# Mixer tokens ordered by 16 grid columns, and neighborhood tiles on 2 or 3 key blocks instead of 4

## The chip, the core and the metric

The kernel runs on one core of one Trainium2 chip. Its engines are TensorE (PE in the profile; its weight loads are PEld), VectorE (DVE), ScalarE (ACT), GpSimd (POOL) and SyncE (SP), which issues the weight loads from memory. The metric is the device time of the core in microseconds, lower is better.

## What is computed

Two blocks of a network on 512 tokens of width 1024, in float32. The first block (attention with a forget gate, a recurrent branch, then a mixture of experts) is not touched by the change. The second block has two layers, each with a mixer and a feed-forward part. The mixer is what matters here. Its tokens are a grid of 8 rows by 64 columns, token = 64 row + column. It has three branches:

```python
def neighborhood_attention(q, k, v, rpb):          # 6 heads of 64
    rows = S // GRID_W                             # 8 rows, GRID_W = 64
    kh = min(NA_KH, rows)                          # 8: all rows
    col_start = jnp.clip(cols - kw // 2, 0, GRID_W - kw)   # kw = 16 columns
    col_idx = col_start[:, None] + jnp.arange(kw)[None, :]
    ...
    s = jnp.einsum('bhqd,bhrqcd->bhqrc', q_row, k_win) * scale + bias
    p = softmax over the 8 x 16 keys of the window
    return jnp.einsum('bhqrc,bhrqcd->bhqd', p, v_win)

def dilated_attention(q, k, v):                    # 6 heads, 3 groups: (128, 1), (512, 4), (2048, 16)
    offs = dilation * jnp.arange(-half, half + 1)  # keys at token distance offs, bias -slope * |offs|
def memory_attention(q, mem_n, w_kv):              # 4 heads, 256 memory tokens

h = rms_norm_2(x, g_pre_mix[l]); proj = h @ w_in[l]
merged = sum over branches of sigmoid(gate) * (branch output @ branch weight)
x = x + rms_norm_2(merged @ w_out[l], g_post_mix[l])
h = rms_norm_2(x, g_pre_ffn[l])                    # then up, conv over 3 tokens, gelu gate, down
```

A query in column c sees all 8 rows but only 16 columns, so with the tokens in order of rows each block of 128 queries (two rows) has some key in every block of 128 keys.

## The kernel before

Activations lie with features on the 128 partitions and tokens in the free dimension: `x`, `h`, `low`, `y` are [128, 8, 512]. A layer is the body of a loop over `LAYERS` = 2 (phase `L`), written out on each engine by hand; the order of each engine's instructions is the order of the code, and engines meet at semaphores only (`Signal`).

A layer begins with the norm `pre_mix`: ScalarE issues the loads of `lvec` (L1241) and of the first bias `nab` (L1242) and squares `x` (L993), TensorE sums (L674), VectorE scales into `low` (`rms_apply`, L1392), ScalarE copies the rounded high part into `h_r` (`high`, L1053) and VectorE forms the rest, `low_r` (`low_part`, L1511). Then come the products for q, k, v. `residual` (L1398, L1401) adds the mixer's output to `x` after the branches, and the feed-forward part follows, whose convolution needs the tokens in their natural order.

Between these stands the attention of the three branches, 24 neighborhood tiles (`na`: 6 heads by 4 blocks of 128 queries), then 8 dilated (`dil`) and 16 memory tiles (`mem`), in the list `TILES["L"]`. `key_chunks(kind, t)` gives the number of key blocks of 128: 4, 6 and 2. The engines are pipelined over tiles. In its round i TensorE issues the score product of tile i (L704, or L701 for `dil`), the transposes of the probabilities of tile i-2, one each block (L715), a product or two of a gate (`gate_products`, L951, 128x512, one in the rounds of `na` tiles and two later), and the value products of tile i-3 (L729). VectorE does for tile i-1 the reciprocal of the row sum (L1432), for tile i the addition of the bias with the row minimum (L1455 for `na`, L1458 and L1460 for `dil`), and for tile i-2 the copy of the transposes out of PSUM (L1474). ScalarE does the exp (L1015), with the row sum read out behind it, and the copy of a finished pair of heads out of PSUM (L1029). GpSimd multiplies the probabilities by the reciprocal (L1861). A score product of tile i waits until the scores of tile i-2 are read; the transposes of a tile wait for GpSimd.

The bias of a head is loaded by ScalarE's queue (L1268) one head ahead into one of two halves of `nab`, [128, 896]. GpSimd then adds the mask of the column window to it (L1900). The four query tiles read it at shifts of 128 columns, 512 wide. The dilated bias of group 0 is read the same way, as 512 neighbours from 3 - t on.

The first block has an attention of its own (phase `A`, kind `fa`) through the same function: 8 heads by 4 query blocks with 1, 2, 3 and 4 key blocks, and no gate products between; every fourth tile a product of L807 for the next head but one.

## Time and profile before

| what | us |
|---|---|
| median of 3 runs | 2861.29 |
| lowest, highest | 2856.5, 2867.2 |
| span of the profiled execution | 2863.9 |
| TensorE busy in it | 2580.2 (90%) |
| VectorE, ScalarE, GpSimd busy | 1157.0, 801.4, 161.5 |

The page gives for the profiled execution its span, from the first to the last instruction; no other time of that execution is shown. Times in the rows further down count from the start of the span. PEclk is the granted clock of TensorE: 1.00 is 2.4 GHz and 0.50 is 1.2 GHz, its two levels. A float32 product shows as two matmul records, and the records of one kind that follow each other are merged with their count. In a row of a timeline the first number is the start, the second the duration; the ends of matmuls are modelled, so what one step takes is read from its start to the start of the next. In layer 0 the neighborhood tiles stand from 1164 to 1238 us, in layer 1 from 2089 to 2163.

### The profile page before, as it was taken

To read this page: it belongs to the slowest core of one execution; us is meant where nothing else is said; L and a number is where in the kernel's file an instruction comes from. 1 tells how busy PE (TensorE), PEld (TensorE's weight loads), DVE (VectorE), ACT (ScalarE), POOL (GpSimd) and SP (SyncE) were. 2 spreads that over 40 slices of the span, in tenths; PEclk is the share of its full clock that TensorE was granted. 3 is DMA by queue.
4 is the path that set the end of the run, shared out by engine and by line. 5 is a ranking of instruction groups with operands and counts; after the bars stand their busy time and mean duration, and the time that the engine had idled before them with its cause. 6 is when DMAs were issued, how large, how long until landed. Compare 5 with 4: busy or idle time off the path is not lost.

```text
span 2863.9 us, 30233 instructions
## 1 busy us (share of the span) xinstructions
PE 2580.2 (90%) x11744; PEld 1956.3 (68%) x11744; DVE 1157.0 (40%) x1664; ACT 801.4 (28%) x1110; POOL 161.5 (6%) x165
## 2 busy tenths in 40 slices
PE   5899886899999489999997999978999999799996
PEld 3674464677777258666875888856866787588885
DVE  5635564000000431354346655333135434655533
ACT  3432313010000142233233433313223323433331
POOL 0001100000000100331000000000033100000000
PEclk8995596899999789899998999989989999899998
DMA  6535041688888413101221222221210122122221
GB/s 238 191 117 206 1 179 50 254 317 319 316 313 311 185 54 117 41 7 59 89 103 45 102 97 95 103 75 67 103 48 1 70 93 88 59 94 98 103 89 45
DMA packets 55809, 353.75 MB, mean 124 GB/s; under 512 B 6016, under 2 KB 6656, under 8 KB 19328
## 3 DMA queue, kind: packets, MB, share of 16 engines
q1 hardware_dynamic: 40464, 294.67, 27.8%
q10 hardware_dynamic: 8640, 30.08, 2.8%
q0 software_dynamic: 6576, 27.26, 2.4%
q8 instruction: 83, 1.36, 0.2%
q14 instruction: 46, 0.38, 0.0%
HBM read 319.49 MB, written 32.51 MB: 123 GB/s over the span
## 4 chain that ended last, share of the span: by engine, by line
PE 44%; issue 40%; DVE 4%; POOL 2%; ACT 2%; DMA 1%; POOLq 0%; DVEq 0%; ACTq 0%
PE lin L870 9%; PE lin L629 7%; PE lin L630 6%; PE lin L643 5%; PE lin L882 5%; PE attn L729 3%; PE score L704 2%; PE trans L715 2%; PE lin L634 2%; POOL y L1861 1%; DVE rstd L1375 1%; PE sums L674 1%; PE sums L669 1%; PE score L701 1%; PE lin L807 0%
## 5 line engine op out<-in xcount | busy, mean ns | idle before, releaser
L629 PE MATMUL lin<-h_r,ring_r 128*128 128x512 f32 x1584 | 626.7, 396 | 46.5 <-ACT h_r L1053 35.7
L630 PE MATMUL lin<-h_r,ring_r 128*128 128x512 f32 x1584 | 622.0, 393 | 0.0
L1505 DVE TENSOR_TENSOR ring_r<-ring,ring_r 128x2048 fp32r<-128x2048 f32 x138 | 316.2, 2292 | 559.1 <-ACT ring_r L1049 559.0
L629 PEld LDWEIGHTS lin<-h_r,ring_r 128*128 128x128 f32 x1584 | 301.0, 190 | 123.7 <-ACT h_r L1053 31.0
L643 PE MATMUL lin<-low_r,ring_r 128*128 128x512 f32 x1392 | 350.1, 391 | 1.9
L630 PEld LDWEIGHTS lin<-h_r,ring_r 128*128 128x128 f32 x1584 | 301.4, 190 | 62.0
L1049 ACT CAST ring_r<-ring 128x2048 fp32r<-128x2048 f32 x138 | 262.4, 1902 | 166.1 <-PE lin L634 105.5
L643 PEld LDWEIGHTS lin<-low_r,ring_r 128*128 128x128 f32 x1392 | 261.3, 188 | 63.2 <-DVE low_r L1511 9.8
L870 PEld LDWEIGHTS lin<-y,ring 128*128 128x128 f32 x2304 | 262.6, 194 | 11.0 <-issue 11.0
L870 PE MATMUL lin<-y,ring 128*128 128x128 f32 x2304 | 263.0, 277 | 2.1 <-DVE y L1741 1.1
L1327 ACT ACTIVATE ob<-lin,lvec 128x512 f32<-128x512 f32 x88 | 68.7, 781 | 301.6 <-PE lin L643 243.7
L1832 DVE SCALAR_TENSOR_TENSOR ob<-lin,lvec,ob 128x511 f32<-128x511 f32 x88 | 66.0, 750 | 196.5 <-ACT ob L1327 194.6
L882 PE MATMUL lin<-ring,ob 128*128 128x512 f32 x288 | 132.8, 604 | 12.0 <-DVE ob L1735 7.8
L1735 DVE TENSOR_TENSOR ob<-gat,lin 128x512 f32<-128x512 f32 x18 | 12.4, 689 | 317.2 <-PE lin L870 317.2
L634 PE MATMUL lin<-big_r,ring_r 128*128 128x512 f32 x352 | 137.2, 390 | 0.6 <-DVE big_r L1511 0.6
L704 PE MATMUL score<-big 64*128 64x512 f32 (+3 forms) x224 | 127.6, 660 | 6.7 <-DVE stat L1455 4.5
L1861 POOL TENSOR_TENSOR y<-y,stat 128x512 f32<-128x512 f32 (+2 forms) x96 | 93.2, 970 | 498.8 <-DVE stat L1432 498.5
L674 PE MATMUL sums<-h,ones_d 128*128 128x512 f32 x96 | 57.9, 760 | 56.9 <-ACT h L993 51.8
L729 PE MATMUL attn<-y,big 128*64 128x128 f32 x704 | 103.3, 286 | 0.0
L882 PEld LDWEIGHTS lin<-ring,ob 128*128 128x128 f32 x288 | 51.7, 189 | 71.8 <-issue 54.7
L729 PEld LDWEIGHTS attn<-y,big 128*64 128x64 f32 x704 | 76.5, 140 | 31.9 <-issue 31.9
L1432 DVE RECIPROCAL stat<-stat 128x1 f32<-128x1 f32 x128 | 20.9, 164 | 184.6 <-PE score L704 133.7
(287 smaller groups left out, 3151.5 us busy)
## 6 DMA issues: line engine op xcount, KB each, us to landing
ring<-in_weights SPq DMA_DIRECT2D x281, 1024.0 KB, 4.9
slots_in<-nab POOLq DMA_DIRECT2D x1, 13312.0 KB, 42.6
y<-slots_in ACTq DMA_DIRECT2D x20, 512.0 KB, 3.6
slots_out<-ob ACTq DMA_DIRECT2D x18, 512.0 KB, 8.7
nab<-in_na_bias ACTq DMA_DIRECT2D x12, 448.0 KB, 3.3
slots_out<-nab POOLq DMA_DIRECT2D x1, 3072.0 KB, 48.4
x<-in_xT ACTq DMA_DIRECT2D x1, 2048.0 KB, 10.9
outT<-x POOLq DMA_DIRECT2D x1, 2048.0 KB, 6.6
```

Of the source, the lines that this page charges most:

```text
L629: pe.matmul(acc, wh, high(k), start=(k == 0), stop=False)
L630: mm = pe.matmul(acc, wl, high(k), start=False, stop=False)
L634: mm = pe.matmul(acc, wh, low(k), start=False, stop=(k == kb - 1))
L643: mm = pe.matmul(acc, wh, low(k), start=False, stop=(k == kb - 1))
L674: mm = pe.matmul(sums[:, 0, 0:n], ones[:, :], src, start=(k == 0), stop=(k == n_k - 1))
L704: mm = pe.matmul(score[:, i % 2, 0:n], q_of(kind)[lo:lo + DH, hp, t * P:(t + 1) * P], k_of(kind)[lo:lo + DH, hp, 0:n], start=True, stop=True)
L729: mm = pe.matmul(attn[lo:lo + DH, o % 2, t * P:(t + 1) * P], v_of(kind, hp, half, t, c0 + c), probsT[name][j % 2][:, c * P:(c + 1) * P], s ...
L870: mm = pe.matmul(acc[:, m * P:(m + 1) * P], wblock(ph, n0 + m * KB + k), xg[e % 2][:, k, :], start=(k == 0), stop=(k == KB - 1))
L882: mm = pe.matmul(acc, hid[e % 2][:, k * P:(k + 1) * P], wblock(ph, n0 + k * KB + 4 * i, 4 * P), start=(k == 0), stop=(k == EB - 1))
L1049: act.copy(ring_r[:, HIGH_SLOT[ph.name][c], :], ring[:, slot, :]).then_inc(*w_high.on(ph, c))
L1505: dve.tensor_tensor(ring_r[:, slot, :], ring[:, slot, :], whole(ring_r[:, HIGH_SLOT[ph.name][c], :]), ALU.subtract).then_inc(*w_low.on(ph, c))
L1861: pool.tensor_tensor(p, p, stat[:, 2, i % 4:i % 4 + 1].to_broadcast([P, n]), ALU.mult).then_inc(*p_ready.on(ph, i))
```

## The change

Within the mixer a token's place becomes 32 a + 4 r + x for row r and column 4 a + x, so a block of 128 places holds 16 columns of all 8 rows. The normed input is written to `y` and brought to the new order by the casts to `h_r` and the subtractions to `low_r` (`by_column`, `by_row`: the same buffer with its free dimension split in three and walked in another order, runs of four words). The residual addition after the mixer brings it back. q, k, v and all branch outputs in between are in the new order.

A query block t of a neighborhood tile now needs the key blocks `NA_KEYS[t]`: from block 0 two, from 0 three, from 1 three, from 2 two. Score product, bias addition, exp, scaling, transposes, copy and value products of the tile are that wide. The bias is stored for three kinds of tile side by side, 2 + 3 + 2 blocks, 896 columns again, with the mask already in it, so GpSimd's addition goes and VectorE waits for the load itself. The dilated bias of group 0 is stored as 128 groups of 7, of which a tile reads 4 each; that of the other groups is loaded once each layer into `tmp`. Small constants (`wf`, `wr`, `route_b`) move into `nab`, which is free until the layers.

```diff
@@ -143,9 +143,29 @@
 }
 
 
+NA_KEYS = [(0, 2), (0, 3), (1, 3), (2, 2)]
+NA_BIAS = [0, 2 * P, 2 * P, 5 * P]
+NA_W = 7 * P
+
+
 def key_chunks(kind, t):
 
-    return {"fa": t + 1, "na": 4, "dil": 6, "mem": 2}[kind]
+    return {"fa": t + 1, "na": NA_KEYS[t][1], "dil": 6, "mem": 2}[kind]
+
+
+def first_key(kind, t):
+
+    return NA_KEYS[t][0] if kind == "na" else 0
+
+
+def by_column(ap):
+
+    return ap.rearrange("p (a r x) -> p r a x", r=ROWS, x=4)
+
+
+def by_row(ap):
+
+    return ap.rearrange("p (r a x) -> p r a x", r=ROWS, x=4)
 
         big, big_r = sb_parts("big", [P, FB, S])
         ob, ob_r = sb_parts("ob", [P, 6, S])
         mem = sb("mem", [P, KB, N_MEM])
-        nab = sb("nab", [P, 2, NA_SLOTS * GRID_W])
-        dil = sb("dil", [P, 2, DIL_W])
+        nab = sb("nab", [P, 2, NA_W])
+        dil = sb("dil", [P, 2, DIL_NEAR])
         tmp = sb("tmp", [P, 2, S])
         gat = sb("gat", [P, 2, S])
         sd = sb("sd", [P, S])
         rstd = sb("rstd", [P, S])
-        consts = sb("consts", [P, 3 * P + GRID_W + 48])
+        consts = sb("consts", [P, 3 * P + 48])
         ones_d = sb("ones_d", [P, P])
         ones = sb("ones", [P, P])
         vec = sb("vec", [P, N_VEC])
         lvec = sb("lvec", [P, N_LVEC])
-        wf = sb("wf", [P, KB, HEADS])
-        wr = sb("wr", [P, KB, N_GROUPS + EXPERTS])
-        route_b = sb("route_b", [P, TT * 20])
+        nab_flat = nab[:, :, :].rearrange("p a b -> p (a b)")
+        wf = nab_flat[:, D:D + KB * HEADS].rearrange("p (a b) -> p a b", a=KB)
+        wr = nab_flat[:, D + 64:D + 224].rearrange("p (a b) -> p a b", a=KB)
+        route_b = nab_flat[:, D + 224:D + 224 + TT * 20]
+        dil_far = tmp[:, 0, :].rearrange("p (a b) -> p a b", a=2)
         slots = sb("slots", [P, 2 * TT], U32)
         weight = sb("weight", [P, 2 * TT])
...
@@ -701,8 +719,9 @@
                             mm = pe.matmul(o, q, k, start=True, stop=True)
                     else:
                         n = key_chunks(kind, t) * P
+                        k0 = first_key(kind, t) * P
                         mm = pe.matmul(score[:, i % 2, 0:n], q_of(kind)[lo:lo + DH, hp, t * P:(t + 1) * P],
-                                       k_of(kind)[lo:lo + DH, hp, 0:n], start=True, stop=True)
+                                       k_of(kind)[lo:lo + DH, hp, k0:k0 + n], start=True, stop=True)
                     mm.then_inc(*qk_done.on(ph, i))
 
                 def turn(j):
@@ -726,7 +745,7 @@
                     total = key_chunks(kind, t)
                     lo = DH * half
                     for c in range(n):
-                        mm = pe.matmul(attn[lo:lo + DH, o % 2, t * P:(t + 1) * P], v_of(kind, hp, half, t, c0 + c),
+                        mm = pe.matmul(attn[lo:lo + DH, o % 2, t * P:(t + 1) * P], v_of(kind, hp, half, t, first_key(kind, t) + c0 + c),
                                        probsT[name][j % 2][:, c * P:(c + 1) * P],
                                        start=(c0 + c == 0), stop=(c0 + c == total - 1))
                     mm.then_inc(*pv_done.on(ph, j))
@@ -1236,9 +1255,13 @@
                 def normed_parts(st):
                     for k in range(KB):
                         act.wait_ge(*normed.by(ph, (st, k)))
-                        high(ph, st, k, h_r[:, k, :], low[:, k, :])
+                        if st == "pre_mix":
+                            high(ph, st, k, by_column(h_r[:, k, :]), by_row(y[:, k, :]))
+                        else:
+                            high(ph, st, k, h_r[:, k, :], low[:, k, :])
 
                 act.dma_start(lvec[:, :], lvec_in[l]).then_inc(lvec_s, 16)
+                act.dma_start(dil_far, far_in).then_inc(far_s, 16)
                 act.dma_start(nab[:, 0, :], na_bias_in[l * NA_HEADS]).then_inc(nab_s, 16)
                 for k in range(KB):
                     square(ph, "pre_mix", k, x[:, k, :], h[:, k, :])
@@ -1398,7 +1421,11 @@
                     dve.scalar_tensor_tensor(tmp[:, k % 2, :], src[:, k, :], lv(g, k), rstd[:, :], ALU.mult,
                                              ALU.mult).then_inc(*upd.on(ph, (st, k)))
                     dve.wait_ge(*upd.by(ph, (st, k)))
-                    dve.tensor_tensor(x[:, k, :], x[:, k, :], tmp[:, k % 2, :], ALU.add).then_inc(*x_new.on(ph, (st, k)))
+                    if st == "post_mix":
+                        dve.tensor_tensor(by_row(x[:, k, :]), by_row(x[:, k, :]), by_column(tmp[:, k % 2, :]),
+                                          ALU.add).then_inc(*x_new.on(ph, (st, k)))
+                    else:
+                        dve.tensor_tensor(x[:, k, :], x[:, k, :], tmp[:, k % 2, :], ALU.add).then_inc(*x_new.on(ph, (st, k)))
 
             ada_chunks = {g[1:]: c for c, g in enumerate(LAST_USE["A"][::PER_CHUNK]) if g[0] == "ada"}
@@ -1450,14 +1477,15 @@
                         dve.tensor_scalar(nm, nm, -1.0, None, ALU.mult).then_inc(*scored.on(ph, i))
                     elif kind == "na":
                         hd = 2 * hp + half
-                        lo = (2 * TT - 2 - 2 * t) * GRID_W
-
-                        dve.tensor_tensor_reduce(p[:, 0:n], s, nab[:, hd % 2, lo:lo + S], -1.0, BIG, ALU.add, ALU.min,
-                                                 nm).then_inc(*scored.on(ph, i))
+                        lo = NA_BIAS[t]
+                        dve.tensor_tensor_reduce(p[:, 0:n], s[:, 0:n], nab[:, hd % 2, lo:lo + n], -1.0, BIG, ALU.add,
+                                                 ALU.min, nm).then_inc(*scored.on(ph, i))
                     elif kind == "dil":
-                        dve.tensor_tensor_reduce(p[:, 0:S], score_flat[:, 0:S], dil[:, half, 3 - t:3 - t + S], -1.0, BIG,
+                        near = dil[:, half, :].rearrange("p (a x) -> p a x", x=7)[:, :, 3 - t:7 - t]
+                        dve.tensor_tensor_reduce(p[:, 0:S].rearrange("p (a x) -> p a x", x=4),
+                                                 score_flat[:, 0:S].rearrange("p (a x) -> p a x", x=4), near, -1.0, BIG,
                                                  ALU.add, ALU.min, nm).then_inc(*score_step.on(ph, (i, 0)))
-                        dve.tensor_tensor_reduce(p[:, S:n], score_flat[:, S:n], dil[:, half, S + 3:], -1.0, BIG,
+                        dve.tensor_tensor_reduce(p[:, S:n], score_flat[:, S:n], dil_far[:, half, :], -1.0, BIG,
                                                  ALU.add, ALU.min, far).then_inc(*score_step.on(ph, (i, 1)))
                         dve.wait_ge(*score_step.by(ph, (i, 1)))
                         dve.tensor_tensor(nm, nm, far, ALU.min).then_inc(*scored.on(ph, i))
@@ -1479,10 +1507,12 @@
                         kind = tl[i][0]
                         dve.wait_ge(*qk_done.by(ph, i))
                         if kind == "na" and i % TT == 0:
-                            dve.wait_ge(*nab_ready.by(ph, i // TT))
+                            dve.wait_ge(nab_s, ph.reg * (16 * NA_HEADS) + 16 * (i // TT + 1))
                         if kind == "fa" and i % TT == 0:
                             hd = i // TT
                             dve.wait_ge(*lin_free[bank_of["A"][f"nc{hd}"]].by(A, f"nc{hd}"))
+                        if i == NA_TILES and name == "L":
+                            dve.wait_ge(far_s, ph.reg * 16 + 16)
                         if i >= 3 and kind != "mem":
                             dve.wait_ge(*t_done.by(ph, ROUNDS_OF[name][i - 3][-1]))
                     if 1 <= i <= n:
@@ -1769,9 +1799,14 @@
                 ph = Phase("L", l)
 
                 def normed_parts(st, g):
-                    rms_apply(ph, st, lambda k: low[:, k, :], lambda k: x[:, k, :], lambda k: lv(g, k), KB)
-                    for k in range(KB):
-                        low_part(ph, st, k, low_r[:, k, :], low[:, k, :], h_r[:, k, :])
+                    if st == "pre_mix":
+                        rms_apply(ph, st, lambda k: y[:, k, :], lambda k: x[:, k, :], lambda k: lv(g, k), KB)
+                        for k in range(KB):
+                            low_part(ph, st, k, by_column(low_r[:, k, :]), by_row(y[:, k, :]), by_column(h_r[:, k, :]))
+                    else:
+                        rms_apply(ph, st, lambda k: low[:, k, :], lambda k: x[:, k, :], lambda k: lv(g, k), KB)
+                        for k in range(KB):
+                            low_part(ph, st, k, low_r[:, k, :], low[:, k, :], h_r[:, k, :])
                 def add_squares(st, k, square, former):
 
...
@@ -1892,20 +1925,7 @@
                         slots[:, i * TT + t:i * TT + t + 1], 0)).then_inc(picked_in[t], 16)
             pool.wait_ge(consts_in, 16 * 4)
             with pool.Fori(0, LAYERS) as l:
-                ph = Phase("L", l)
-
-                def bias(hd):
-                    b = nab[:, hd % 2, :].rearrange("p (a b) -> p a b", b=GRID_W)
-                    pool.wait_ge(nab_s, l * (16 * NA_HEADS) + 16 * (hd + 1))
-                    pool.tensor_tensor(b, b, window.unsqueeze(1).to_broadcast([P, NA_SLOTS, GRID_W]),
-                                       ALU.add).then_inc(*nab_ready.on(ph, hd))
-
-                def next_bias(i):
-                    if i == 0:
-                        bias(0)
-                    if i % TT == 2 and i // TT + 1 < NA_HEADS:
-                        bias(i // TT + 1)
-                attention(ph, extra=next_bias)
+                attention(Phase("L", l))
 
 
+            out.append(np.where(ok, -slopes[2 * g + b] * np.abs(dist).astype(np.float32), np.float32(MASKED)))
+    return np.stack([out[0], out[3]], axis=1), np.stack([out[1], out[2], out[4], out[5]], axis=1).reshape(P, 2, DIL_FAR)
 
 
 def neighborhood_bias(rpb):
 
 
-    c = np.arange(GRID_W)
-    reach = 2 * NA_KW - 1
-    pad = np.zeros((*rpb.shape[:3], 2 * GRID_W - 1), np.float32)
-    lo = GRID_W - 1 - (NA_KW - 1)
-    pad[..., lo:lo + reach] = rpb
-    full = pad[..., GRID_W - 1 + c[None, :] - c[:, None]]
-    full = full.transpose(0, 1, 3, 2, 4)
-    both = np.concatenate([full[:, :, :, 1:], full[:, :, :, :-1]], axis=2)
-    return np.ascontiguousarray(both).reshape(-1, P, NA_SLOTS * GRID_W)
+    tiles = []
+    for t in (0, 1, 3):
+        c0, n = NA_KEYS[t]
+        col, row = (v[:, None] for v in columns(np.arange(t * P, (t + 1) * P)))
+        key_col, key_row = (v[None, :] for v in columns(np.arange(c0 * P, (c0 + n) * P)))
+        start = np.clip(col - NA_KW // 2, 0, GRID_W - NA_KW)
+        inside = (key_col >= start) & (key_col < start + NA_KW)
+        across = np.where(inside, key_col - col + NA_KW - 1, 0)
+        tiles.append(np.where(inside, rpb[:, :, key_row - row + NA_KH - 1, across], np.float32(MASKED)))
+    return np.ascontiguousarray(np.concatenate(tiles, axis=-1)).reshape(-1, P, NA_W)
 
 
```

On TensorE, in the rounds of neighborhood tiles away from the ends, one round before (`lin` is the bank of the gate, `ring_r` its weights, `attn` the value products' bank; L695 and L713 are waits on a register's value):

```order
L704 MATMUL score<-big 128x512
L713 REGISTER_ALU
L715 MATMUL trans<-consts,y 128x128 x4
L951 MATMUL lin<-h_r,ring_r 128x512
L729 MATMUL attn<-y,big 64x128 x4
L695 REGISTER_ALU
```

and two rounds of the change at the same place, tiles with three key blocks in the score product:

```order
L723 MATMUL score<-big 128x384
L732 REGISTER_ALU
L734 MATMUL trans<-consts,y 128x128 x2
L970 MATMUL lin<-h_r,ring_r 128x512
L748 MATMUL attn<-y,big 64x128 x3
L713 REGISTER_ALU
L723 MATMUL score<-big 128x384
L732 REGISTER_ALU
L734 MATMUL trans<-consts,y 128x128 x2
L970 MATMUL lin<-h_r,ring_r 128x512
L748 MATMUL attn<-y,big 64x128 x2
```

No instruction changes its place; the products are narrower and there are fewer transposes and value products.

On ScalarE, at the start of a layer, before (`h` takes the squares of `x`):

```order
L1241 DMA lvec<-in_lvec 128x232
L1242 ISA
L1242 DMA nab<-in_na_bias 128x896
L993 ACTIVATE h<-x 128x512 x8
```

and in the change:

```order
L1263 DMA lvec<-in_lvec 128x232
L1264 DMA tmp<-in_dil_far 128x512
L1265 ISA
L1265 DMA nab<-in_na_bias 128x896
L1012 ACTIVATE h<-x 128x512 x8
```

One load has come in ahead of the squares.

## Rows read from the trace of the kernel before

**Rows 1.** The page, its header: the span of the profiled execution.
```profile
span 2863.9 us, 30233 instructions
```

**Rows 2.** Stretches: start:end, length, busy us (instructions) of PE, PEld, DVE, ACT, POOL, clock.
```profile
214.00:339.00 125.00, 117.48 (x304) 59.88 (x304) 71.69 (x197) 27.41 (x75) 23.07 (x32) 0.50 0.30 121
...
1166.00:1182.00 16.00, 13.38 (x34) 6.91 (x34) 7.79 (x19) 5.08 (x11) 6.19 (x5) 0.50 0.20 73
1183.00:1237.00 54.00, 54.00 (x280) 31.95 (x280) 25.49 (x76) 15.72 (x39) 27.42 (x23) 1.00 0.10 31
```

**Rows 3.** Timeline (start, us, engine, line, tiles), one neighborhood round at full clock.
```profile
1185.85 1.12 PE L704 MATMUL score<-big 64*128 64x512 f32 x2
...
1186.90 0.66 PE L715 MATMUL trans<-consts,y 128*128 128x128 f32 x4
...
1187.09 0.67 DVE L1455 CUSTOM_DVE_ANT_0 y<-score,nab 128x512 f32<-128x512 f32 x1
...
1187.31 0.48 PE L951 MATMUL lin<-h_r,ring_r 128*128 128x512 f32 x1
...
1187.72 1.09 PE L729 MATMUL attn<-y,big 128*64 128x128 f32 x8
1187.80 0.72 ACT L1015 ACTIVATE y<-y,stat 128x512 f32<-128x512 f32 x1 [2.08 <-DVE stat L1455]
...
1188.43 0.19 ACT L1015 ACTIVATION_READ_ACCUMULATOR y<-y,stat 128x1 f32 x1
...
1188.74 1.12 PE L704 MATMUL score<-big 64*128 64x512 f32 x2
```

**Rows 4.** Timeline, TensorE, one memory round (two key blocks) at full clock.
```profile
1290.87 0.70 PE L704 MATMUL score<-big 64*128 64x256 f32 x2
...
1291.49 0.44 PE L715 MATMUL trans<-consts,y 128*128 128x128 f32 x2
...
1291.69 0.71 PE L951 MATMUL lin<-low_r,ring_r 128*128 128x512 f32 x2
...
1292.33 0.65 PE L729 MATMUL attn<-y,big 128*64 128x128 f32 x4
...
1292.91 0.70 PE L704 MATMUL score<-big 64*128 64x256 f32 x2
```

**Rows 5.** Timeline, TensorE, neighborhood rounds at the lower clock.
```profile
1168.70 2.07 PE L704 MATMUL score<-big 64*128 64x512 f32 x2 [2.46 <-DVE stat L1455]
...
1174.41 1.11 PE L715 MATMUL trans<-consts,y 128*128 128x128 f32 x4
...
1177.78 2.07 PE L704 MATMUL score<-big 64*128 64x512 f32 x2
1179.78 1.11 PE L715 MATMUL trans<-consts,y 128*128 128x128 f32 x4
```

**Rows 6.** Timeline, TensorE, first block's attention: a score product of three blocks.
```profile
298.19 1.65 PE L704 MATMUL score<-big 64*128 64x384 f32 x2
...
299.76 0.47 PE L715 MATMUL trans<-consts,ob 128*128 128x128 f32 x1
```

**Rows 7.** Timeline: the first transposes of the stage and the first dilated score product.
```profile
1170.93 1.11 PE L715 MATMUL trans<-consts,y 128*128 128x128 f32 x4 [0.16 <-POOL y L1861]
...
1237.82 2.17 PE L701 MATMUL score<-big 64*128 64x512 f32 x6
```

**Rows 8.** Timeline: the issue of the first bias load at the layer's start.
```profile
1008.21 0.35 ACTq L1242 DMA_DIRECT2D nab<-in_na_bias  x1
```

**Rows 9.** Copies of attention outputs in the layers: ns min/median/max, first and last start.
```profile
L1029 ACT COPY ob<-attn x12: 564/577/1063, 1203.0 to 2247.3; 128x512 f32<-128x512 f32 x12
```

**Rows 10.** Groups by form: the residual additions, busy us and mean ns.
```profile
L1401 DVE TENSOR_TENSOR x<-x,tmp 128x512 f32<-128x512 f32 x32 | 22.1, 692 | 1.1
```

**Rows 11.** Timeline, layer 0: the eight casts and eight low parts of pre_mix.
```profile
1024.39 5.26 ACT L1053 CAST h_r<-low 128x512 fp32r<-128x512 f32 x8 [4.21 <-DVE low L1392]
...
1028.92 4.89 DVE L1511 TENSOR_TENSOR low_r<-low,h_r 128x512 fp32r<-128x512 f32 x8
```

49 lines of the change are left out of this document (21 added, 28 removed).

## Prediction

> **What bounds the kernel now.** I read the page's header first, for the span [rows 1], then a table of stretches with the granted clock [rows 2], then the instructions of single tiles in order of time. The change acts on the mixer, which runs twice. In the neighborhood stage of one layer TensorE is busy 54.00 of 54.00 us at full clock, with VectorE at 25.49, ScalarE at 15.72 and GpSimd at 27.42 [rows 2]. So what TensorE issues there sets the time, and work taken from the other three is worth nothing by itself. The second thing to see is the clock. It is at 0.50 when the stage begins (16 us from 1166) and is 1.00 from 1183 on, so it came back between 1182 and 1183. And in the first block's attention, 214 to 339 us, it stays at 0.50 for 125 us although TensorE is busy 117.48 of them [rows 2]. That row decides how much of the gain is kept.
>
> **TensorE work of one tile.** At full clock a tile of four key blocks goes: score product 1185.85, transposes 1186.90, gate product 1187.31, value products 1187.72, next score product 1188.74 [rows 3]. That is 1.05 + 0.41 + 0.41 + 1.02 = 2.89 us. What a block costs is seen on the memory tiles, which have two blocks: score 1290.87 to 1291.49 = 0.62, transposes to 1291.69 = 0.20, value products 1292.33 to 1292.91 = 0.58 [rows 4]. Two blocks less save 0.43 + 0.21 + 0.44 = 1.08 us, so a block is 0.54. The change takes the 24 tiles of a layer from 4 to 2, 3, 3, 2 blocks, 1.5 less on average: 0.81 us, and a tile becomes 2.89 - 0.81 = 2.08 us. The gate product stays in every tile and costs what it did.
> At the lower clock the tile takes 1174.41 to 1179.78 = 5.37 us, its score product 2.00 [rows 5]. A score product of three blocks takes 298.19 to 299.76 = 1.57 there [rows 6], 0.43 less, just twice the 0.215 of full clock. I take the whole block at twice 0.54: 5.37 - 1.5 x 1.08 = 3.75 us a tile. Each microsecond that the stage spends at the lower clock therefore costs 1 - 2.08/3.75 = 0.45 us.
>
> **The stage.** Its first transposes start at 1170.93 and the first dilated score product at 1237.82 [rows 7], 66.9 us for 21 full rounds and a first short one (transposes and gate, 0.82 at full clock). Check: 21 x 2.89 + 0.82 = 61.5, plus 12 us at the lower clock (1170.93 to about 1182.9) at 1 - 2.89/5.37 = 0.46, gives 67.0. After the change: 21 x 2.08 + 0.7 = 44.4, plus 0.45 H, with H the time from the first transposes until the clock is back. These transposes come behind the third score product (two products from 1168.70, 2.07 long, at the lower clock [rows 5]) and may start about 0.7 earlier, since it loses a block (0.43) and the first score operation before it shrinks by two blocks (an estimate, 0.25). Gain of a layer: 66.9 + 0.7 - 44.4 - 0.45 H = 23.2 - 0.45 H.
> **H is not in the trace.** The new tiles lie between two things that it shows: the old tiles, after which the clock came back in 12 us, and the first block's attention, with 1, 2, 3, 4 blocks (2.5 on average, just the new mean) but no gate product, where it did not come back in 125 us [rows 2]. With H = 12 a layer gains 17.8; at the lower clock throughout (21 x 3.75 + 1.1 = 79.9) it loses 12.3; break-even is H = 52. The new tile keeps the gate product, so I put it nearer to the old ones and take H = 28: 10.6 us a layer, 21.2 for both.
> The page "TensorE: Matmul & The Clock Gate" of the Trainium skill (What's actually happening) says that the default state is throttled and that activity releases it. By that the busy stage would soon be back at full clock and the result is rival B below; the row of the first block's attention does not agree with it as it stands.
>
> **Do the other engines keep up?** From the start of the transposes, which is the end of a score product, a tile of four needs until 1188.62: score operation from 1187.09, exp from 1187.80, its accumulator read until then, 1.72 us [rows 3]. With three blocks the two long operations (0.67 and 0.72) lose about a fifth each, some 0.25: 1.47. The shortest time between two ends of score products in the new order is 0.20 + 0.41 + 0.58 + 0.62 = 1.81. It fits, with 0.3 to spare. The 12 mask additions on GpSimd go; TensorE waits for nothing in those 54.00 us, so they are worth 0. VectorE now waits for the bias load itself, with its own reciprocal, score operation and copy queued behind it; the load is asked for four tiles earlier, 8 us at the new pace, so 0.
> **Added: one DMA issue** on ScalarE's queue ahead of each layer's first squares, 0.35 us like the one beside it [rows 8], on the path: 0.7 for both. Its 256 KB are first read at the dilated tiles, 229 us later. The bounds are 0 and 1.1.
> **Added: rearranged operands**, all of 128x512: 16 casts (ScalarE), 16 residual additions and 16 low parts (VectorE), and 16 dilated score operations reading bias in runs of four. No row shows runs of four words. The nearest is the copy of an attention output, which for the dilated one writes with a stride of four words: the longest is 1063 ns beside a median of 577 [rows 9], a factor of 1.84. If runs cost that much, an addition of 0.69 [rows 10] grows by 0.58, a low part (4.89/8 = 0.61, [rows 11]) by 0.51, and a dilated score operation, 0.67 like that of the neighborhood, by 0.56; 16 of each on the path make 9.3 + 8.2 + 9.0 = 26.5. The casts (5.26/8 = 0.66) would grow to 1.21 but run beside low parts that end late anyway. The other end is 0, since a gain from a less regular operand is excluded. I take 0: in each run of four the words are neighbours as in a plain operand, and the row at 1.84 has none that are.
> "SBUF — State Buffer" of the Trainium skill (Specifications (TRN2)) has 16-byte lines and asks for at least two hits a line. That also prices runs of four fp32 words at nothing; the dilated bias, which starts at any word, touches more lines than it did. No run here shows that.
>
> **Sum.** 2863.9 [rows 1] - 21.2 + 0.7 = 2843.4 for the profiled execution. Its span is 2.6 above the median of 2861.3, so the median should go to 2841.
>
> **Rivals.**
> A, the forecast (0.40): the clock comes back late in the stage, H from 20 to 45, a layer gains 14.2 to 3.0. 2833 to 2856, mostly below 2847.
> B (0.22): it comes back as early as now. 2 x 17.8 - 0.7 = 34.9, 2826. For it: tiles without a gap, and the gate product in each. Against it: every tile has less behind it than now.
> C, the other side (0.10): it stays down through the neighborhood tiles of both layers, as in the first block. 2 x 12.3 + 0.7, and some 2 us of dilated tiles, is 27 to 28 more: 2889. It decides from H = 52 on. For it: the 125 us at 0.50. Against it: in those, no gate product.
> D (0.13): one layer early, the other not at all. 17.8 - 12.3 - 0.7 = 4.8 gained, 2856.
> E (0.10): the rearranged operands cost what the strided copy did. 2841 + 26.5 = 2867.
> F (0.05): VectorE, ScalarE and GpSimd in turn become the bound of the short rounds, a wait of 0.3 in every second tile of both layers, 7 us: 2848.
>
> **How the numbers follow.** This kernel can be told from no change at about 0.5%, 14.3 us. Faster: A's 0.33, B's 0.22, F's and E's 0.05 make 0.60. Within: A's 0.07, D's 0.13, E's and F's 0.09, 0.29. Slower: C and a little of E, 0.11. The range 2820 to 2872 takes in A, B, D, F and the mean of E and leaves out C and the tails.
>
> **What would show it.** Right: score products of 256 and 384 columns, a tile of about 2.08 us at full clock and 3.75 at the lower one, and the new stage 44.4 + 0.45 H. Look at the clock of that stage in both layers before anything else. The additions, low parts and dilated score operations should stay at 0.69, 0.61 and 0.67; a number near 1.2 is E. A TensorE idle for VectorE or GpSimd within the neighborhood tiles is F. A clock back within 15 us in both layers makes 2841 too high; one that is down until the dilated tiles makes it too low.

## The result, and the profile after

| | before | changed |
|---|---|---|
| median, us (5 runs each) | 2865.58 | 2837.59 |
| lowest, highest | 2856.5, 2868.02 | 2831.02, 2849.51 |
| span of the profiled execution | 2863.9 | 2835.8 |

The ratio is 0.9913, 95% interval 0.9888 to 0.9938. The forecast was 2841, with 2820 to 2872 around it. Such a ratio leaves out the runs that are more than 1.5% above the fastest of their kernel, which matters for this kernel, as the first experiment shows.

The stretches of the neighborhood stage, in the columns of [rows 2], first of layer 0 (two rows) and then of layer 1 (two rows):

```profile
1169.00:1208.00 39.00, 39.00 (x110) 22.64 (x111) 11.49 (x44) 7.96 (x25) 8.02 (x11) 0.50 0.13 42
1209.00:1230.00 21.00, 21.00 (x107) 12.30 (x106) 10.12 (x43) 7.14 (x22) 7.50 (x11) 1.00 0.08 23
2088.00:2095.00 7.00, 7.00 (x21) 4.06 (x21) 3.09 (x12) 1.91 (x6) 2.27 (x3) 0.50 0.06 23
2097.00:2135.00 38.00, 38.00 (x194) 22.41 (x194) 18.36 (x75) 13.22 (x39) 13.64 (x19) 1.00 0.12 38
```

TensorE is busy all the time in each of them, and the clock does something else in the two layers: in layer 0 it is at 0.50 for the first 39 us of the stage, in layer 1 for the first 8. Before, it was about 12 in both.

The edges of the stage on TensorE (timeline: start, duration, engine, line, tiles), first transposes and first dilated score product of layer 0, then the same of layer 1:

```profile
1168.88 0.69 PE L734 MATMUL trans<-consts,y 128*128 128x128 f32 x2
...
1230.64 2.16 PE L719 MATMUL score<-big 64*128 64x512 f32 x6
...
2087.47 0.69 PE L734 MATMUL trans<-consts,y 128*128 128x128 f32 x2
...
2135.26 2.16 PE L719 MATMUL score<-big 64*128 64x512 f32 x6
```

The stage of layer 0 takes 1230.64 - 1168.88 = 61.8 us, where [rows 7] have 66.9. That of layer 1 takes 2135.26 - 2087.47 = 47.8, before 66.7. The transposes start 5.98 us after the first score product of the stage, before 6.88. So the two stages give 5.1 + 18.9 = 24.0 us and the earlier transposes 1.8. The spans differ by 28.1. Of the 2.3 that are left, 1.5 lies ahead of the layers, where no work was taken away.

Two rounds at full clock, TensorE:

```profile
1210.07 0.91 PE L723 MATMUL score<-big 64*128 64x384 f32 x2
1210.91 0.44 PE L734 MATMUL trans<-consts,y 128*128 128x128 f32 x2
1211.10 0.47 PE L970 MATMUL lin<-h_r,ring_r 128*128 128x512 f32 x1
1211.51 0.65 PE L748 MATMUL attn<-y,big 128*64 128x128 f32 x4
1212.09 0.70 PE L723 MATMUL score<-big 64*128 64x256 f32 x2
1212.71 0.55 PE L734 MATMUL trans<-consts,y 128*128 128x128 f32 x3
```

The score product of three blocks takes 0.84 and that of two 0.62, two transposes 0.19, the value products of two blocks 0.58, as in [rows 4]. The whole round takes 2.02. The same round at the lower clock:

```profile
1181.35 1.65 PE L723 MATMUL score<-big 64*128 64x384 f32 x2
1182.93 0.69 PE L734 MATMUL trans<-consts,y 128*128 128x128 f32 x2
1183.27 0.78 PE L970 MATMUL lin<-h_r,ring_r 128*128 128x512 f32 x1
1183.97 1.12 PE L748 MATMUL attn<-y,big 128*64 128x128 f32 x4
1185.02 1.22 PE L723 MATMUL score<-big 64*128 64x256 f32 x2
```

It takes 1.58 + 0.34 + 0.70 + 1.05 = 3.67 us.

The rows that answer to [rows 10], in groups by form (busy us and mean ns behind the bar), with the other operands that the change rearranges:

```profile
L1425 DVE TENSOR_TENSOR x<-x,tmp 128x512 f32<-128x512 f32 x16 | 11.1, 692 | 0.5
L1428 DVE TENSOR_TENSOR x<-x,tmp 128x512 f32<-128x512 f32 x16 | 11.1, 692 | 0.5
...
L1072 ACT CAST h_r<-y 128x512 fp32r<-128x512 f32 x24 | 14.6, 619 | 13.9 <-DVE y L1415 13.1
L1072 ACT CAST h_r<-low 128x512 fp32r<-128x512 f32 x24 | 14.1, 616 | 12.3 <-DVE low L1415 11.6
...
L1541 DVE TENSOR_TENSOR low_r<-low,h_r 128x512 fp32r<-128x512 f32 x24 | 14.7, 688 | 0.0
L1541 DVE TENSOR_TENSOR low_r<-y,h_r 128x512 fp32r<-128x512 f32 x16 | 9.8, 686 | 0.0
...
L1485 DVE CUSTOM_DVE_ANT_1 y<-score,dil 128x512 f32<-128x512 f32 x16 | 10.8, 672 | 0.0
```

and from the timeline the row of the changed kernel that answers to the second of [rows 11], the eight low parts of layer 0:

```profile
1027.54 4.90 DVE L1541 TENSOR_TENSOR low_r<-y,h_r 128x512 fp32r<-128x512 f32 x8
```

L1425 is the residual addition with rearranged operands, L1428 the plain one of the feed-forward part: 692 ns each. The low parts from `y` (rearranged, 686) and from `low` (plain, 688) are alike, and eight of them take 4.90 where they took 4.89. So are the casts (of the 24 from `y`, 16 are rearranged), and the dilated score operation with its runs of four is at 672 beside 671 before.

### The profile page after: what moved, and what is told of

Read it like the earlier page. It is cut to its first block, busy times and chain, and to the rows that moved or that the text cites. A ratio compares the mean times of both kernels' runs of the same rounds, so it can differ in the third digit from the quotient of the medians.

```text
span 2835.8 us, 29781 instructions
## 1 busy us (share of the span) xinstructions
PE 2549.3 (90%) x11528; PEld 1939.9 (68%) x11528; DVE 1139.0 (40%) x1664; ACT 793.1 (28%) x1110; POOL 120.7 (4%) x153
## 3 DMA queue, kind: packets, MB, share of 16 engines
q1 hardware_dynamic: 40464, 294.67, 28.1%
## 4 chain that ended last, share of the span: by engine, by line
PE 77%; DVE 7%; issue 3%; ACT 3%; DMA 1%; POOL 0%; ACTq 0%; DVEq 0%; POOLq 0%
PE lin L647 15%; PE lin L648 14%; PE lin L661 11%; PE lin L889 9%; PE lin L901 5%; PE attn L748 4%; PE lin L652 3%; PE score L723 3%; PE trans L734 2%; PE sums L692 2%; DVE rstd L1398 1%; PE score L719 1%; PE lin L970 1%; PE lin L669 1%; PE lin L671 1%
## 5 line engine op out<-in xcount | busy, mean ns | idle before, releaser
L661 PEld LDWEIGHTS lin<-low_r,ring_r 128*128 128x128 f32 x1392 | 261.3, 188 | 61.5 <-DVE low_r L1541 7.8
L652 PE MATMUL lin<-big_r,ring_r 128*128 128x512 f32 x352 | 137.2, 390 | 0.6 <-DVE big_r L1541 0.6
L1894 POOL TENSOR_TENSOR y<-y,stat 128x256 f32<-128x256 f32 (+2 forms) x96 | 77.6, 808 | 1183.5 <-DVE stat L1459 1183.5
L723 PE MATMUL score<-big 64*128 64x256 f32 (+2 forms) x224 | 115.5, 607 | 7.6 <-DVE stat L1481 5.3
L647 PE MATMUL lin<-big_r,ring_r 128*128 128x512 f32 x224 | 88.4, 395 | 5.0 <-ACT big_r L1072 4.7
L748 PE MATMUL attn<-y,big 128*64 128x128 f32 x560 | 91.5, 298 | 0.0
## 6 DMA issues: line engine op xcount, KB each, us to landing
x<-in_xT ACTq DMA_DIRECT2D x1, 2048.0 KB, 10.7
```

The lines of the kernel that those rows point to most:

```text
L647: pe.matmul(acc, wh, high(k), start=(k == 0), stop=False)
L652: mm = pe.matmul(acc, wh, low(k), start=False, stop=(k == kb - 1))
L661: mm = pe.matmul(acc, wh, low(k), start=False, stop=(k == kb - 1))
L723: mm = pe.matmul(score[:, i % 2, 0:n], q_of(kind)[lo:lo + DH, hp, t * P:(t + 1) * P], k_of(kind)[lo:lo + DH, hp, k0:k0 + n], start=True, s ...
L748: mm = pe.matmul(attn[lo:lo + DH, o % 2, t * P:(t + 1) * P], v_of(kind, hp, half, t, first_key(kind, t) + c0 + c), probsT[name][j % 2][:, ...
L1894: pool.tensor_tensor(p, p, stat[:, 2, i % 4:i % 4 + 1].to_broadcast([P, n]), ALU.mult).then_inc(*p_ready.on(ph, i))
```

## Experiments

The question was what decides how long the clock stays down, since this alone separated the rivals, and whether the rearranged operands are free. All kernels below are the changed one with a small edit, unless the text says that it is the kernel before. A filler product is a product of 128x512 with all 128 rows, whose result is overwritten before anybody reads it. The stage is, as above, the time from its first transposes to the first dilated score product. The edit for the neighborhood stage:

```diff
+FILL = {"A": lambda i: 0, "L": lambda i: 12 if i == 1 else 0}
...
                     if i < n:
                         qk(i)
+                    for u in range(FILL[name](i)):
+                        pe.matmul(attn[:, 1, :], h_r[:, 0, 0:P], h_r[:, u % KB, :], start=True, stop=True)
```

**The changed kernel once more, a_again.** No edit.

> The changed kernel once more, unaltered. Clock theory: the time at 1.2 GHz in the neighborhood stage, H, differs between the layers of one execution (39 and 8 us in the first trace) and between executions, each stage takes 44.4 + 0.45 H within 1 us, and the runs scatter over some 20 us. Rival (layer 0 is slow for a reason of its own): 62 and 48 us again, H 39 and 8 again.

Ten runs: 2828.4, 2835.8, 2837.7, 2861.6, 2874.2, 2875.4, 2876.0, 2894.2, 2897.4, 2897.8; the kernel before on the same chip had 16 between 2851.2 and 2866.0, median 2862.05. The ratio is 0.9933 (0.9896 to 0.9971), but the median of all ten is 2874.8, which is 12.7 above the kernel before: on this chip the change gained in three runs and lost in six. The profiled run, 2897.4, shows what the longest ones are. Stretches of both stages, columns as above:

```profile
1168.00:1247.00 79.00, 79.00 (x220) 44.89 (x221) 22.85 (x88) 15.73 (x48) 16.05 (x22) 0.50 0.09 28
2110.00:2189.00 79.00, 79.00 (x221) 44.88 (x221) 22.80 (x88) 15.80 (x48) 16.05 (x22) 0.50 0.09 28
```

and the end of the stage of layer 0 on TensorE:

```profile
1247.88 2.99 PE L719 MATMUL score<-big 64*128 64x512 f32 x6
```

The clock is at 0.50 through both stages and on into the dilated tiles, 102.4 us each time, while TensorE has no gap in 79 of 79 us. From the first transposes (1167.91) to the first dilated score product (1247.88) it is 79.97 us; the prediction's rival C had 79.9. The time is 2897.4 and C had 2889. So C is another outcome of the same program on the same chip as the short runs. The scatter is 69 us, not the 20 of the expectation.

Traces of the other nine were not taken, but their mean granted clocks are on record and fall as the time grows: 0.919 to 0.922 in the three from 2828 to 2838, 0.910 at 2861.6, 0.904 at 2875, 0.895 to 0.897 in the longest three. An estimate from them, with the two profiled executions as its ends (0.919 with 58 us at the lower clock in the two layers, 0.895 with 205): the run at 2861.6 fits one stage at the lower clock throughout and the other back early, which is rival D, and the three at 2875 fit one stage throughout and the other back after some 40 us.

**Filler at the start of the neighborhood tiles, a_fill, and the same in the kernel before, b_fill.** Twelve products in round 1, where TensorE otherwise waits 2.9 us for VectorE.

> The changed kernel, with 12 products of 128x512 (from h_r, into the second bank of attn, read by nobody) put between the second and the third score product of the mixer, where TensorE waits 2.87 us for the first score operation. Clock theory (what is lost in the neighborhood stage against 44.4 us is only time at 1.2 GHz): the clock does not fall there, first transposes to first dilated score product take 44.4 us in both layers instead of 61.8 and 47.8, and the kernel takes 2835.8 - 17.4 - 3.4 = 2815 us. Rival (the narrower tiles wait for another engine in layer 0, or the clock falls anyway): the two stages stay near 62 and 48 and the time is that of the changed kernel plus up to 2 x 2.7 us.

> The kernel before with the same 12 products at the same place. Clock theory: the stage takes 61.5 us in both layers instead of 66.9 and 66.7, the kernel 2863.9 - 10.6 = 2853 us; the difference to the changed kernel with the 12 products is then what the change is worth at full clock, 2 x 17.1 plus 2 x 0.5 to 0.9 for the start of the stage, 35 to 36 us. Rival (the products only add work): 66.9 + up to 2.7 us a layer.

| | median (range) | ratio to before | stage, both layers |
|---|---|---|---|
| a_fill | 2817.7 (2813.9 to 2854.4, 4 runs) | 0.9884 (0.9811 to 0.9958) | 44.17, 44.17 |
| b_fill | 2851.4 (2846.4 to 2857.5, 7 runs) | 0.9963 (0.9947 to 0.9979) | 61.53, 61.44 |

TensorE at the start of the stage in a_fill, timeline:

```profile
1161.50 1.44 PE L727 MATMUL score<-big 64*128 64x256 f32 x4 [0.55 <-ACT big L1290]
1162.87 4.44 PE L764 MATMUL attn<-h_r 128*128 128x512 f32 x12
1167.24 0.91 PE L727 MATMUL score<-big 64*128 64x384 f32 x2
1168.08 0.44 PE L738 MATMUL trans<-consts,y 128*128 128x128 f32 x2
```

and two stretches of a_fill, in the filler and in the stage, and one of b_fill, all of layer 0:

```profile
1163.00:1166.00 3.00, 3.00 (x7) 2.35 (x8) 2.65 (x4) 1.57 (x3) 0.00 (x0) 0.50 0.69 289
1168.00:1212.00 44.00, 44.00 (x223) 25.99 (x223) 21.52 (x88) 15.14 (x45) 15.92 (x22) 1.00 0.14 48
```

```profile
1173.00:1233.00 60.00, 59.98 (x310) 35.34 (x309) 29.28 (x87) 18.07 (x45) 32.46 (x27) 1.00 0.10 32
```

In the trace of a_fill the clock fell at 1162.6 and was back 3.4 us later, ahead of the stage. The stage then takes 44.17 where the prediction has 44.4 for H = 0; in the old kernel it takes the 61.5 of the prediction's check. With the clock up in both, the change is worth 2851.4 - 2817.7 = 33.7 us. That is what the narrower tiles bring; what the changed kernel loses of it, it loses to the clock. In the old kernel the filler saves 10.7, the price of its 12 us at the lower clock in two layers (2 x 5.4).

**Plain operands, a_fill_plain.** a_fill with `by_column` and `by_row` returning their operand unchanged, so the tokens are in the wrong order for the branches, with every instruction of its old size.

```diff
-    return ap.rearrange("p (a r x) -> p r a x", r=ROWS, x=4)
+    return ap
...
-    return ap.rearrange("p (r a x) -> p r a x", r=ROWS, x=4)
+    return ap
```

> The changed kernel with the twelve filler products at the start of the neighborhood tiles (as in a_fill), and with by_column and by_row returning their operand as it is: the casts, the subtractions and the residual additions of the mixer walk plain rows of 512 words. The tokens are then in the wrong order for the branches, but every instruction has the size that it had. My theory (runs of four words cost nothing): the same time as a_fill, 2817, within 5 us, with additions at 692 ns, casts at 619, low parts at 687. Rival E (the runs cost what the strided copy does): 17 us less for the additions and low parts, 2800, since here only these are made plain and the dilated score operations keep their runs of four.

Four of five runs at 2814.2, 2816.7, 2820.1 and 2825.4, a_fill's at 2813.9, 2817.6 and 2817.9. Nothing of the 17 us of rival E is there. The additions take 692, the casts 619, the low parts 689 ns. The fifth run, 2859.2, is the profiled one, and in it the filler failed. Stretches of layer 0 behind the filler, and then of the stage:

```profile
1165.00:1168.00 3.00, 2.92 (x12) 2.07 (x12) 2.65 (x4) 1.59 (x2) 0.00 (x0) 1.00 0.71 300
1168.00:1171.50 3.50, 2.30 (x8) 1.05 (x9) 1.61 (x7) 1.93 (x6) 1.44 (x2) 1.00 0.47 131
1172.00:1248.00 76.00, 76.00 (x213) 42.98 (x212) 21.46 (x83) 14.63 (x44) 15.17 (x21) 0.50 0.08 25
```

Here the clock had not fallen yet when the filler came. The twelve products took 3.0 us and were over by 1168, TensorE waited again behind them (2.30 busy of 3.50), the clock fell at 1171.7, and it was not back for 95.6 us, though the tiles left TensorE no gap. a_fill's run of 2854.4 has a like excess, 37 us beside 41, and a like mean clock, 0.913 beside 0.912; its trace was not taken.

It isn't shown that the early filler is the cause. In b_fill it ran at full clock too, there was a wait behind it as well, and the clock stayed at 1.00:

```profile
1167.37 3.01 PE L745 MATMUL attn<-h_r 128*128 128x512 f32 x12
...
1172.38 0.66 PE L719 MATMUL trans<-consts,y 128*128 128x128 f32 x4 [0.94 <-POOL y L1867]
```

In every other layer traced with this filler the clock was down for at most 6.8 us around it and back before the first transposes.

**Is it the gate product? a_nogate and fill_nogate.** The prediction put the new tile near the old ones because of the gate product. Both kernels move the gate products out of the neighborhood rounds; fill_nogate has a_fill's filler besides.

```diff
-    GATE_AT.append(GATE_AT[-1] + (1 if _i < NA_TILES else 2))
+    GATE_AT.append(GATE_AT[-1] + (0 if _i < NA_TILES else 3))
```

> The changed kernel without gate products in the neighborhood rounds; the dilated and memory rounds have three each instead of two, so none is left out. The prediction held that the gate product brings the clock back. If so, the clock stays at 0.50 through the 24 tiles as in the first block's attention, a round takes 3.75 - 0.70 = 3.05 us and the stage 64 us in both layers. If the gate product does not matter, the clock comes back as in the changed kernel, a round at full clock takes 2.08 - 0.41 = 1.67 us and the stage 36 to 50 us.

> a_fill with the gate products of the neighborhood rounds moved to the dilated and memory rounds (three there, none here). My claim in the prediction was that the gate product in each tile keeps the clock up. In a_fill it was up over the whole stage, with gate products. If the claim holds, the clock falls back within the stage although TensorE goes on without a gap, as it did within 7 us in fa_one: tiles of 3.3 us (3.75 less 0.43) for most of the 21 rounds, stage 60 to 68 us. Rival (any dense work holds it): the clock stays at 1.00 and the stage is 44.2 less 21 x 0.4 = 35.5 to 36 us. The dilated and memory rounds take the 8 us back in either case, so the whole says little: 2815 to 2850.

a_nogate: 2887.0 us, stages of 70.6 at 0.50 throughout, not the 64 of the expectation. Since a_again stayed at 0.50 too, with gate products, this tells nothing of them but their price, 80.0 - 70.6 = 9.4 in 22 rounds, 0.43 each. fill_nogate: 2812.1, stages of 39.28 and 39.28:

```profile
1165.00:1203.00 38.00, 37.76 (x195) 21.68 (x193) 20.37 (x85) 14.74 (x44) 15.02 (x22) 1.00 0.15 50
```

The clock is at 1.00 to the end with no gate product in the stage. So the gate product isn't needed to hold it, and this part of the reasoning falls. Whether it helps to bring the clock back is not shown. (The stage is 39.3 and not 35.5. From the transposes of three blocks to the value products it is now 0.48 where it was 0.30 to the gate product, so taking it away saves 0.23 in such a round and not 0.41. What takes the rest was not tried.)

**The first block's attention: fa_one, fa_burst, a_best, fa_two, a_both.** It runs at 0.50 from start to end in both kernels. All have filler in the neighborhood stage too (fa_two and a_both that of a_hold, below), and add filler here, ahead of the score products, into the bank that the score product then writes; a_best is both of the first two together. The last column of the table counts the same products put ahead of the second head's mask product (the product of L807 in the kernel before):

```diff
                         n = key_chunks(kind, t) * P
+                        for u in range(FA_FILL(i) if kind == "fa" else 0):
+                            pe.matmul(score[:, i % 2, :], h_r[:, 0, 0:P], h_r[:, u % KB, :], start=True, stop=True)
```

| | `FA_FILL(i)` | in the gap at 214 us |
|---|---|---|
| fa_one | `1` | 0 |
| fa_burst | `4 if i < 4 else 0` | 12 |
| a_best | `4 if i < 4 else 1` | 12 |
| fa_two | `4 if i % 4 == 0 else 2` | 12 |
| a_both | `16 if i == 4 else 4 if i > 4 and i % 4 == 0 else 1 if i > 4 else 0` | 0 |

> a_fill with one more product of 128x512, which nobody reads, ahead of each of the 32 score products of the first block's attention; it takes the part that the gate product has in a neighborhood tile. In a_fill that attention runs at 1.2 GHz from the first tile to the last (about 222 to 342 us). My claim in the prediction was that the gate product is what lets the clock come back. If so, the clock comes back within the attention: TensorE then needs 32 x (1.84 + 0.22) = 66 us, VectorE 72, and the stage ends near 300 instead of 342, the whole 40 us under a_fill: 2775. Rival (a product a tile does not matter, the gap-ridden start decides): the clock stays at 0.50 and the stage is 32 x 0.43 = 14 us longer, 2830.

> a_fill with filler products of 128x512 that nobody reads at the start of the first block's attention only: twelve where TensorE waits for the running sum (214 to 219 us), then four ahead of each of the first four score products, none after. If the level of the clock is decided at the start and held by any steady work (theory 1): the clock is back by about 230 us and stays at 1.00 through 32 tiles that have no gate product; the stage ends near 295 and the whole is about 45 us under a_fill: 2770. If tiles without a gate product cannot hold it (theory 2, the gate product keeps the clock): it falls again within the stage, and the whole is 2817 plus up to 7 us of filler, 2817 to 2824.

> Both together: twelve filler products in the gap, four ahead of each of the first four score products and one ahead of each later one in the first block's attention, and twelve at the start of the neighborhood tiles. If the clock follows the work that TensorE is given: 1.00 in both attentions, TensorE 66 us of the first one, VectorE 72: stage about 75 to 80 instead of 120, whole 2770 to 2780. If it does not come back in the first attention: 2817 + 14 + 7 = 2838.

> Filler products in the first block's attention: twelve in the gap at 214 us, then two ahead of each score product and four in each fourth tile, behind the mask product of the next head, which uses 8 of 128 rows of the array (in fa_one the clock was back for 6.8 us twice and fell again in the stretch that has this product). If enough full-width products hold the clock: TensorE 59 + 80 x 0.215 = 76 us, the stage some 80 instead of 120, the whole 2775 to 2785. If not: 80 x 0.43 = 34 us longer, 2850. The neighborhood tiles are as in a_hold.

fa_burst, 2821.0: the clock is at 0.83 on average from 212 to 222 and at 0.50 from there on; theory 1 falls. It stayed down although four of the full-width products stand ahead of each of the first four score products, from 217.7 on:

```profile
219.50:340.00 120.50, 118.38 (x304) 60.64 (x304) 66.94 (x189) 25.67 (x73) 21.96 (x31) 0.50 0.25 103
```

fa_one, 2824.2, lies between its two expectations: the clock came back twice (at 240 and 271) and fell again after 6.8 us, in the midst of dense work. Its stretches:

```profile
230.00:240.00 10.00, 10.00 (x27) 5.07 (x25) 5.05 (x15) 2.49 (x7) 1.44 (x2) 0.50 1.02 422
240.50:246.90 6.40, 6.37 (x27) 3.06 (x26) 4.34 (x14) 1.74 (x5) 1.44 (x2) 1.00 1.02 420
248.00:267.00 19.00, 19.00 (x46) 9.41 (x46) 9.77 (x28) 4.07 (x12) 2.97 (x5) 0.50 0.11 42
```

TensorE is busy 6.37 of 6.40 us at 1.00, and yet the clock falls. So it isn't a wait that makes it fall here. What lies in that stretch is the mask product of the next head (L838 there, 8 rows of 128), 1.05 us long. a_best, with one product a tile besides the bursts, had one such rise and came to 2833.3 (2829.5 to 2841.3, 4 runs; ratio 0.9905, 0.9881 to 0.9930): the filler cost more than it gave. fa_two, 2821.4, puts four behind each mask product and two elsewhere:

```profile
219.00:284.00 65.00, 65.00 (x154) 32.58 (x154) 28.26 (x81) 12.94 (x34) 9.03 (x13) 0.51 0.49 201
286.00:336.00 50.00, 48.17 (x212) 25.91 (x212) 36.28 (x102) 13.55 (x39) 12.12 (x17) 1.00 0.00 1
```

Once the clock was back, at 285, it stayed for the last 50 us, through three mask products. What that gave, the filler of the 65 us before took. Neither of the two times expected, near 2780 and 2850, came.

a_both was to bring it back early by one dense burst and hold it with fewer.

> a_hold with filler products in the first block's attention too, placed by what fa_one and fa_two showed: sixteen in a row ahead of the fifth score product, when the tiles follow each other without gaps (6.9 us at 1.2 GHz), then one ahead of each score product and four in each fourth tile behind the mask product. If a dense stretch of full-width products brings the clock back and these few hold it: clock at 1.00 from about 240 us to the end of the stage near 337; four tiles take 11.5 us (fa_two's 11.9 us in its last 50 us, less three fillers) instead of 15.4, so seven groups save 27 and the burst costs 5: 20 to 25 us under a_hold, 2795 to 2800. Rival 1 (one product a tile does not hold it, as in fa_one): the clock falls at a mask product, the stage costs 5 + 7 x 3.0 = 26 us more, 2845. Rival 2 (at full clock VectorE's chain of some 12 us a group bounds the stage): 2800 to 2805.

2824.7 (2818.8 to 2827.7, 4 runs; ratio 0.987, 0.9851 to 0.9889). The burst, and the fall, on TensorE:

```profile
230.73 5.75 PE L728 MATMUL score<-h_r 128*128 128x512 f32 x16
236.41 0.49 PE L731 MATMUL score<-big 64*128 64x128 f32 x2
...
256.28 0.44 PE L742 MATMUL trans<-consts,ob 128*128 128x128 f32 x2
256.64 0.43 PE L756 MATMUL attn<-ob,big 128*64 128x128 f32 x2
257.01 1.12 PE L838 MATMUL lin<-tmp,consts 8*128 8x512 f32 x2
258.06 1.64 PE L728 MATMUL score<-h_r 128*128 128x512 f32 x4
```

The clock came back within 4 us of the start of sixteen full-width products (at 234.7), it held over one mask product (245) and fell behind the second (258.6), with a score product of four blocks (64 rows) and the mask product (8 rows) ahead. It was back at 306 and held to the end of the tiles. The burst part of the expectation came true and the holding part went the way of rival 1, whose 2845 is 20 too high since the clock was back for the last 31 us. The whole is no shorter than a_hold's. No version gained in this attention.

**A version that beats both kernels, a_hold.** Twelve filler products in round 1 and eight in round 4 of the neighborhood stage.

```diff
-"L": lambda i: 12 if i == 1 else 0
+"L": lambda i: {1: 12, 4: 8}.get(i, 0)
```

> The changed kernel with twelve filler products in round 1 and eight in round 4 of the neighborhood tiles, no others. In the profiled run of a_fill_plain the twelve were over at full clock (by 1168 us), the clock fell in the gap behind them (at 1171.7) and stayed down for 95.6 us; a_fill had one run in four at 2854 that this would explain. If a second burst among the first tiles brings the clock back each time: all runs within 2813 to 2825, median 2820 (a_fill's 2817 and 2 x 8 x 0.215 = 3.4 us), ratio near 0.985. Rival (the bursts can miss as before): again one run in four or five near 2855.

2819.6 (2815.4 to 2823.6, 4 runs), ratio 0.9853 (0.9829 to 0.9876), stages of 46.04 and 46.06 at full clock. No run among the four is near 2855. fa_two and a_both have the same filler here, and with them it is none in nine; with the first burst alone two runs in sixteen had such an excess (a_fill, a_fill_plain). That is a sign and no proof, and in the traces of these versions the clock was back before the second burst came. It is 18 under the changed kernel's better set of runs and 55 under the median of its ten, on other chips. The medians of the kernel before on these chips agree within about 4 us.

## Why the prediction came out as it did

The median of 2837.6 lies 3.4 under the forecast. The prices in the sum were right, but for the small one of the DMA issue. That the clock came out near what I had assumed was luck of these five runs: ten more of the same kernel have a median of 2874.8.

- **TensorE bounds the stage:** right, 21.00 of 21.00 and 38.00 of 38.00 us busy. F is refuted: there was no wait for another engine in these stretches.
- **0.54 a block, 2.08 and 3.75 a tile:** right. 21 rounds and the first took 44.17 at full clock (a_fill) against 44.4, and 79.97 at the lower (a_again) against 79.9.
- **Stage = 44.4 + 0.45 H:** right. In the profiled execution H was 1208.3 - 1168.9 = 39.4 and 2095.8 - 2087.5 = 8.3; the formula gives 62.1 and 48.1, measured 61.8 and 47.8. In a_again H is 98 in both layers, beyond the end of the stage. The transposes came 0.9 earlier, not 0.7.
- **H = 28 in both layers:** the mean was 23.9 in the profiled execution, but not for the reason given. H isn't a size of the kernel but differs between the layers of one execution and between executions: 8, 39 and twice 98 were seen in four stages. What decides it, no run here shows. The step that failed is "the new tile keeps the gate product, so I put it nearer to the old ones": fill_nogate holds the clock without any. And A to D, set out as cases that exclude each other, are outcomes of one kernel; their chances should have been shares of runs. Ten runs had three at 2828 to 2838 (between B and A), one at 2862 (near D), three at 2874 to 2876 (between D and C), three at 2894 to 2898 (C), where I gave C 0.10. The break-even at H = 52 is what makes this matter: by the estimate above ten of the twenty stages of these runs lie beyond it.
- **The rule of the Trainium skill** ("TensorE: Matmul & The Clock Gate", What's actually happening: throttled by default, activity releases) gave rival B. The trace of a_again disagrees as far as being busy is meant: 79 of 79 us busy at 0.50. In a_both the clock came back within 4 us of the start of sixteen full-width products, but in fa_burst it did not in tiles with four such products each.
- **Rearranged operands, 0 (E 26.5):** right, 692 beside 692 ns and 2814 to 2825 us for the plain version. "SBUF — State Buffer" of the Trainium skill (Specifications (TRN2), two hits a line of 16 bytes) had it so, and the trace agrees, for the dilated bias too, whose runs start at any word: 672 ns beside 671. The low parts stayed at the 0.61 that the prediction had divided out of a row of eight (4.90 beside 4.89 us); the mean of a single one is 686 ns.
- **The added DMA issue, 0.35 a layer:**

```profile
1006.57 0.46 ACTq L1264 DMA_DIRECT2D tmp<-in_dil_far  x1
1007.20 0.34 ACTq L1265 DMA_DIRECT2D nab<-in_na_bias  x1
```

  It takes 0.46, with 0.63 to the next, above the 0.35 of [rows 8]. From the issue of `lvec` to the first square it is now 1.40 in layer 0 and 1.88 in layer 1, before 0.92 and 1.21: 1.15 for both, above the forecast's 0.7 and a little above its bound of 1.1. On the whole it is lost among other things: from the layer's start to the first score product it is 0.34 longer in layer 0 and 0.34 shorter in layer 1, so it can't be told from nothing there.
- **GpSimd's additions, 0:** nearly right. The engine's busy time fell from 161.5 to 120.7 us, in part because its scaling is narrower too, and only TensorE's 0.16 us of waiting for it ahead of the first transposes [rows 7] went with it.

## What to carry to other kernels

Where a stage is bound by TensorE and starts behind a gap, ask first at which clock it runs and price the change at both levels; a cut that thins the products can leave the clock down for longer and lose at 1.2 GHz what it gained at 2.4. A few full-width products that nobody reads, put where TensorE waits ahead of such a stage, were worth 18 to 55 us here in the changed kernel and 11 in the one before; in the first block's attention they gained nothing. Where the outcomes are drawn anew at each execution, give them as shares of runs, and read the time of every run: one profile is one draw.

## What the runs showed of the hardware

- TensorE can stay at 1.2 GHz though it is always busy: 79 of 79 us (a_again), and almost so, 118.4 of 120.5 us, in the first block's attention (fa_burst, from 219.5 on).
- It can fall there from 2.4 GHz without a gap: 6.37 of 6.40 us busy before the fall (fa_one), with a product of 8 of 128 rows in the last microseconds before it, and likewise in a_both at 258.6. Whether the rows are the cause wasn't tried by itself: no run has the same tiles without the mask product.
- The clock was back within 4 us of the start of sixteen products of 128x512 with 128 rows in a row (a_both). In tiles whose score products use 64 rows it was back after 8, 39 or 98 us, and not at all in the 120 us of the first block's attention without filler. With four full-width products ahead of each of four such tiles it was not back either (fa_burst). What decides it stays open.
- The same program on the same chip took from 2828.4 to 2897.8 us, with a mean granted clock of 0.922 in the shortest and 0.895 to 0.897 in the three longest.
- Runs of four fp32 words cost VectorE and ScalarE nothing that shows (692 beside 692, 619 beside 616, 672 beside 671 ns), where the copy with single words at a stride of four in [rows 9] took 1.84 times the median.
